# Layer-norm reciprocal deviation: square root on ScalarE and reciprocal on VectorE, in place of logarithm and exponential on ScalarE

## The chip, the cores and the metric

The kernel runs on one core of one Trainium2 chip. The metric is the device time of one launch in microseconds (us), median of several runs. Lower is better.

## The reference

One step of a two-layer streaming encoder over 1024 prompt tokens and 32 sample tokens (1056 columns together), model width 1024, all in float32. Layer 0 is a gated DeltaNet mixer and a convolutional feed-forward network (FFN), layer 1 is multi-head latent attention and an FFN of the same shape. Each of the four sub-layers ends in the same way, and that is what the change touches:

```
x = layer_norm(ALPHA * x + (1 + gate) * mix, ln_g, ln_b)

def layer_norm(x, g, b):
    mu = mean(x);  var = mean(square(x - mu))       # over the 1024 features
    return (x - mu) * rsqrt(var + 1e-5) * g + b
```

The next sub-layer reads `hin = x * (1 + scale) + shift` with its own conditioning terms.

## The kernel before, in words

The residual stream X stays in SBUF with features on the partitions: 8 blocks of 128 features by 1056 columns. The columns are worked in three chunks of 352 (`CHS`, ch = 0, 1, 2). Chunk 2 holds the last 320 prompt columns and the 32 sample columns, so an operation with a gain per sequence is issued twice there. Each float32 product on TensorE is three passes over a high and a low part (WH, WL of the weights, HH, HL of the activations, lines 374, 377 and 378).

The order of the work is written out by hand for each engine, and semaphores tie the engines together. No planner reorders it. Weights arrive on SyncE's DMA queue in slabs of 1024 columns (RAW), ScalarE rounds them to WH (`split_hi`, line 365), and GpSimd or VectorE forms WL (`split_lo`, line 370).

The four layer norms are q = 0 (after the DeltaNet), 1 (after the first FFN), 2 (after attention) and 3 (after the second FFN, at the end of the program). For q = 0, 1, 2 the first products of the next sub-layer follow at once. One norm works like this, chunk by chunk:

- `pe_mean` (lines 495 and 498): a product with a matrix of ones puts the column sum on all partitions, from partial sums that GpSimd has added (`pool_sum`, line 619) and the last block of X, which VectorE has just updated (`update` in `vec_proj`, line 1634, or in `vec_ffn`, line 2154).
- `vec_center` (line 640): VectorE subtracts the mean, two blocks at a time.
- `act_squares` (line 537): ScalarE squares, and `pe_var` (line 506) sums the squares, 8 products by a chunk.
- `act_rstd` (lines 539 to 545): ScalarE takes Ln of variance plus eps, waits for itself, and takes Exp of minus half of it. The semaphore `std_rdy` counts two steps for each chunk, 6 for each norm. The tile LN_R stands in the profile as RST.
- `vec_scaled` (lines 651 and 655): VectorE multiplies the centred X by gain and LN_R, which gives the tile TBN (q < 3) or X (q = 3). It waits for the second step of `std_rdy`.
- q < 3: `act_upper` (line 555) makes HH from TBN, `vec_low` (line 677) makes HL from TBN and HH. TensorE's next products of that chunk (`pe_head`) wait for both.
- q = 3: `vec_shift` (line 665) and `act_affine` (line 572) add the offset, and SyncE stores y.

On VectorE the order in `vec_tail` is, for q < 3: the updates of chunk 2, with the centring of chunk 1 among them or ahead of them. Then the first four blocks of `vec_scaled(0)`, *and only then* the last update of chunk 2. Then the rest of `vec_scaled(0)`, a weight slab, `vec_low(0)`, a second slab, the centring of chunk 2, and for chunks 1 and 2 in turn `vec_scaled` and `vec_low`. For q = 3 all updates come first, then two blocks of `vec_scaled(0)`, the centring of chunk 2, the other six blocks, `vec_shift(0)`, and `vec_scaled` and `vec_shift` of chunks 1 and 2.

On TensorE `pe_tail` puts the variance of chunk 0 in chunk 2 of the last products, then the mean of chunk 2 and the variance of chunk 1. `pe_head` starts the next sub-layer, with the variance of chunk 2 after its first product of chunk 0.

The latent projections of layer 1 (`rms_root`, line 2364, and `vec_norm`, line 2403) already take their reciprocal deviation as Sqrt on ScalarE and a reciprocal on VectorE, on the same 128 x 352 float32 shape.

Of the kernel before, what the change touches and what calls it, by code (L numbers as in the profile page):

```python
# [7 lines left out]
D = 1024  # L8
# [4 lines left out]
CHS = [(0, 352), (352, 352), (704, 352)]  # L13
# [95 lines left out]
def build(nc, xT, cT, cB, ws, wada0, wada, par, cst, s0, cs, msk, pckv, pkpe, y, o_gdn, o_gcv, s_gdn, o_fcv, o_ckv, o_kpe):  # L109
    fp32, f32r = mybir.dt.float32, mybir.dt.float32r  # L110
    ALU, ACT, AX = mybir.AluOpType, mybir.ActivationFunctionType, mybir.AxisListType
    ds = bass.ds
    ctx = ExitStack()
    with ctx:
# [13 lines left out]
        def sb(name, shape, dt=fp32):  # L128
            return at(name, shape, dt)[0]
# [3 lines left out]
        def sem(name):  # L133
            sems[name] = ctx.enter_context(nc.semaphore(name))
            return sems[name]
# [14 lines left out]
        EPS = sb("EPS", [128, 3])  # L150
# [70 lines left out]
        LN_SQ, LN_TB, LN_R, LN_SUM = [], [], [], []  # L221
# [32 lines left out]
        for i in range(3):  # L254
# [36 lines left out]
        PS = ctx.enter_context(nc.psum_tensor("PS", [128, 8, 512], fp32))  # L291
# [33 lines left out]
        sum_rdy, mean_ps, cen_rdy, lsq_rdy, var_ps, std_rdy, nrl_rdy, x_rdy = (sem(n) for n in (  # L325
            "sum_rdy", "mean_ps", "cen_rdy", "lsq_rdy", "var_ps", "std_rdy", "nrl_rdy", "x_rdy"))
# [40 lines left out]
        def split_lo(e, n, u):  # L367

            need(e, hi_done, n + 1)
            e.tensor_tensor(WL[u][:, :], RAW[:, u, :], WH[u][:, :].bitcast(fp32), ALU.subtract).then_inc(lo_done, 1)  # L370
# [39 lines left out]
        def pieces(c0, cw):  # L410

            out = []
            for st, (a, b) in enumerate((PRO, SAMP)):
                lo, hi = max(a, c0), min(b, c0 + cw)
                if lo < hi:
                    out.append((lo, hi - lo, st))
            return out
# [68 lines left out]
        def slab_after(q):  # L486

            return (S_F0, S_KV, S_F1, None)[q]
# [50 lines left out]
        def act_rstd(a, q, ch):  # L539

            cw = CHS[ch][1]
            a.wait_ge(var_ps, 3 * q + ch + 1)
            a.activation(LN_R[q][ch][:, 0:cw], PS[:, 3 + ch, 0:cw], ACT.Ln, scale=1.0 / D, bias=EPS[:, 0:1]).then_inc(std_rdy, 1)
            a.wait_ge(std_rdy, 6 * q + 2 * ch + 1)
            a.activation(LN_R[q][ch][:, 0:cw], LN_R[q][ch][:, 0:cw], ACT.Exp, scale=-0.5).then_inc(std_rdy, 1)

        def act_upper(a, q, ch):

# [29 lines left out]
        def act_ln(a, q):  # L578

            n = slab_after(q)  # L580
            act_squares(a, q, 0)
            act_rstd(a, q, 0)
            act_squares(a, q, 1)
            if q == 3:
                act_squares(a, q, 2)
                act_rstd(a, q, 1)
                act_affine(a, q, 0)
                act_rstd(a, q, 2)
                act_affine(a, q, 1)
                act_affine(a, q, 2)  # L590
                return
            split_hi(a, n, n % 2)
            act_upper(a, q, 0)
            split_hi(a, n + 1, (n + 1) % 2)
            act_rstd(a, q, 1)
            act_squares(a, q, 2)
            act_upper(a, q, 1)
            act_rstd(a, q, 2)
            act_upper(a, q, 2)
# [34 lines left out]
        def vec_center(v, q, ch, b):  # L634

            c0, cw = CHS[ch]
            if b == 0:
                v.wait_ge(mean_ps, 3 * q + ch + 1)
                mixed(v, q, KB - 1, ch)
            v.scalar_tensor_tensor(X[:, b:b + 2, c0:c0 + cw], PS[:, ch, 0:cw].unsqueeze(1).to_broadcast([128, 2, cw]), -1.0 / D,  # L640
                                   X[:, b:b + 2, c0:c0 + cw], ALU.mult, ALU.add).then_inc(cen_rdy, 1)

        def vec_scaled(v, q, ch, b0, b1):

            c0, cw = CHS[ch]
            hs = HS[q]
            v.wait_ge(std_rdy, 6 * q + 2 * ch + 2)
            v.wait_ge(cen_rdy, 12 * q + 4 * ch + 4)
            for b in range(b0, b1):
                if q == 3:  # L650
                    ins = v.scalar_tensor_tensor(X[:, b, c0:c0 + cw], X[:, b, c0:c0 + cw], PAR[:, P_LNG + KB * q + b:P_LNG + KB * q + b + 1],
                                                 LN_R[q][ch][:, 0:cw], ALU.mult, ALU.mult)
                else:
                    for x, w, st in pieces(c0, cw):
                        ins = v.scalar_tensor_tensor(LN_TB[q][ch][:, b, x - c0:x - c0 + w], X[:, b, x:x + w],
                                                     LGB[:, MODE[hs], 0, b, st:st + 1], LN_R[q][ch][:, x - c0:x - c0 + w], ALU.mult, ALU.mult)
                if b % 2 == 1:
                    ins.then_inc(nrl_rdy if q == 3 else tmp_rdy, 1)

        def vec_shift(v, ch):  # L660

            c0, cw = CHS[ch]
            v.wait_ge(nrl_rdy, 6 + 5 * ch + 4)
            for b in range(KB // 2, KB):
                ins = v.tensor_scalar(X[:, b, c0:c0 + cw], X[:, b, c0:c0 + cw], PAR[:, P_LNB + KB * 3 + b:P_LNB + KB * 3 + b + 1], None, ALU.add)
            ins.then_inc(nrl_rdy, 1)

        def vec_low(v, q, ch):

            c0, cw = CHS[ch]  # L670
            hs = HS[q]
            for b in range(KB):
                if b % 2 == 0:
                    v.wait_ge(hh_rdy, hin_count(hs, ch) - 3 + b // 2)
                    v.wait_ge(tmp_rdy, tmp_count(hs, ch) - 3 + b // 2)
                for x, w, st in pieces(c0, cw):
                    ins = v.scalar_tensor_tensor(HL[:, b, x:x + w], LN_TB[q][ch][:, b, x - c0:x - c0 + w], LGB[:, MODE[hs], 1, b, st:st + 1],
                                                 HH[:, b, x:x + w].bitcast(fp32), ALU.add, ALU.subtract)
            ins.then_inc(hl_rdy, 1)

        def vec_tail(v, q, update, groups, cut, first=iter(())):

            for ch in range(NCH):
                for i in range(groups):
                    if ch == 2 and i == groups - 1 and q < 3:
                        vec_scaled(v, q, 0, 0, 4)
                    update(ch, i)
                    if ch == 0:
                        next(first, None)
                        continue  # L690
                    if groups == 2 and i == 0:
                        for b in range(0, KB, 2):
                            vec_center(v, q, ch - 1, b)
                    elif groups == KB and 1 <= i <= 4:
                        vec_center(v, q, ch - 1, 2 * (i - 1))
                for _ in first:
                    pass
            if q == 3:
                vec_scaled(v, q, 0, 0, 2)
                for b in range(0, KB, 2):  # L700
                    vec_center(v, q, 2, b)
                vec_scaled(v, q, 0, 2, KB)
                vec_shift(v, 0)
                for ch in (1, 2):
                    vec_scaled(v, q, ch, 0, KB)
                    vec_shift(v, ch)
                return
            n = slab_after(q)
            vec_scaled(v, q, 0, 4, KB)
            split_lo(v, n, n % 2)  # L710
            vec_low(v, q, 0)
            split_lo(v, n + 1, (n + 1) % 2)
            for b in range(0, KB, 2):
                vec_center(v, q, 2, b)
            for ch in (1, 2):
                vec_scaled(v, q, ch, 0, KB)
                vec_low(v, q, ch)

# [232 lines left out]
        def past(e, s, count):  # L951

            if count > 0:
                e.wait_ge(s, count)
# [1152 lines left out]
        def vec_ffn(v, l, s, g0):  # L2107
# [233 lines left out]
            mix(NP - 2, beside())  # L2341
            last_lower(1, 0)
            vec_tail(v, 2 * l + 1, lambda ch, m: update(NP - 1, KB * ch + m, m, ch, last_bank), KB, 2, within())

        def no_hin(ch):
# [1146 lines left out]
```

## Time and profile before

| | |
|---|---|
| median of 3 runs | 3078.75 us |
| runs | 3074.51 to 3082.51 us |
| profiled execution, its own time | 3073.38 us |
| its span | 3071.6 us |
| TensorE busy | 95% of the span |
| VectorE busy | 74% |
| ScalarE busy | 40% |
| GpSimd busy | 36% |
| mean granted TensorE clock | 0.98 |

The span runs from the first to the last instruction of the profiled execution. Engines work side by side, so their shares don't add up to 100%. In the rows below a timeline merges like instructions in sequence into one row, and gives in brackets the time the engine sat idle before it and whose work ended that idle time.

### The profile page before, as it was taken

Reading aid. Unit: us, or ns where it says so; the run is one execution under the profiler, and the core shown is the slowest. Engines: PE = TensorE matmul, PEld = TensorE weight load, DVE = VectorE, ACT = ScalarE, POOL = GpSimd, SP = SyncE. Lnnn points to the kernel's source line nnn. Section 1 sums busy time; section 2 is a strip of 40 time slices with the busy share of each in tenths; the row PEclk is TensorE's granted clock in tenths of the full one; section 3 lists DMA queues with packets and bytes.
Section 4 is the critical chain, followed back from the end, with each engine's and each line's share of the span. In section 5 each row is a group of like instructions: output and inputs, shape, how many; then the busy total and the mean of one; then the engine's idle time right before and its main releaser. Section 6 shows DMA issues by size and latency. Waiting matters only on the chain.

```text
span 3071.6 us, 51912 instructions
## 1 busy us (share of the span) xinstructions
PE 2921.7 (95%) x18516; PEld 2795.7 (91%) x18516; DVE 2266.1 (74%) x3438; ACT 1218.5 (40%) x2348; POOL 1099.6 (36%) x727
## 2 busy tenths in 40 slices
PE   7999989999999999999999888989999999999997
PEld 5999986999898999999998877878889999999996
DVE  7999975777629788788787655646348778878777
ACT  4333334555416433333333644444346333333334
POOL 2333444666332344433344121111223433334432
PEclk9999989999999999999999999999999999999999
DMA  7454663211111111111111210101211111111111
GB/s 274 166 183 171 215 226 114 64 52 34 36 42 41 43 48 48 52 44 48 48 48 36 96 53 29 36 22 71 85 35 35 49 55 41 51 44 48 49 54 58
DMA packets 87017, 225.75 MB, mean 73 GB/s; under 512 B 9436, under 2 KB 41124, under 8 KB 85860
## 3 DMA queue, kind: packets, MB, share of 16 engines
q1 hardware_dynamic: 46948, 139.10, 13.2%
q10 hardware_dynamic: 39936, 84.86, 8.0%
q8 instruction: 85, 1.39, 0.2%
q14 instruction: 48, 0.39, 0.0%
HBM read 192.59 MB, written 31.35 MB: 73 GB/s over the span
## 4 chain that ended last, share of the span: by engine, by line
PE 77%; DVE 11%; issue 5%; ACT 4%; DMA 1%; ACTq 1%; POOL 0%; SPq 0%; DVEq 0%; POOLq 0%
PE PS L374 14%; PE PS L377 13%; PE PS L378 13%; PE PS L1735 6%; PE PS L1739 6%; PE PS L1738 6%; DVE CV L3292 4%; PE PS L981 2%; PE PS L2600 2%; PE PS L997 2%; PE PS L506 2%; DVE PS L861 1%; PE PS L2584 1%; PE PS L1053 1%; DVE X L2154 1%
## 5 line engine op out<-in xcount | busy, mean ns | idle before, releaser
L370 POOL TENSOR_TENSOR WL<-RAW,WH 128x1024 fp32r<-128x1024 f32 x193 | 508.7, 2636 | 1029.4 <-ACT WH L365 1029.3
L374 PE MATMUL PS<-HH,WH 128*128 128x352 f32 x2120 | 701.4, 331 | 38.4 <-issue 13.0
L378 PE MATMUL PS<-HH,WL 128*128 128x352 f32 x2120 | 688.2, 325 | 0.0
L377 PE MATMUL PS<-HL,WH 128*128 128x352 f32 x2120 | 687.5, 324 | 0.0
L374 PEld LDWEIGHTS PS<-HH,WH 128*128 128x128 f32 x2120 | 403.5, 190 | 55.9 <-issue 44.7
L377 PEld LDWEIGHTS PS<-HL,WH 128*128 128x128 f32 x2120 | 404.6, 191 | 1.8
L378 PEld LDWEIGHTS PS<-HH,WL 128*128 128x128 f32 x2120 | 403.8, 190 | 0.0
L365 ACT ACTIVATE WH<-RAW 128x1024 fp32r<-128x1024 f32 x199 | 210.4, 1057 | 461.7 <-PE PS L374 360.7
L2154 DVE SCALAR_TENSOR_TENSOR X<-PS,ADA,X 128x352 f32<-128x352 f32 (+1 forms) x704 | 319.2, 485 | 88.0 <-PE PS L378 83.6
L378 PE MATMUL PS<-FH,WL 128*128 128x352 f32 x960 | 310.7, 324 | 0.0
L374 PE MATMUL PS<-FH,WH 128*128 128x352 f32 x960 | 310.4, 323 | 0.0
L377 PE MATMUL PS<-FL,WH 128*128 128x352 f32 x960 | 310.3, 323 | 0.0
L2126 DVE SCALAR_TENSOR_TENSOR CF<-UF,PSF,CF 128x1060 f32<-128x1060 f32 x176 | 291.2, 1709 | 0.0
L861 DVE CUSTOM_DVE_ANT_0 PS<-ADR,CB 128x1024 f32<-128x1024 f32 x144 | 196.6, 1365 | 6.8 <-DMA ADR<-wada 2.3
L374 PEld LDWEIGHTS PS<-FH,WH 128*128 128x128 f32 x960 | 180.6, 188 | 0.3
L377 PEld LDWEIGHTS PS<-FL,WH 128*128 128x128 f32 x960 | 180.5, 188 | 0.0
L378 PEld LDWEIGHTS PS<-FH,WL 128*128 128x128 f32 x960 | 180.0, 187 | 0.0
L1557 POOL TENSOR_TENSOR AM<-M,CST 128x1024 f32<-128x1024 f32 (+1 forms) x61 | 135.7, 2241 | 69.3 <-PE PS L981 50.7
L3292 DVE SCALAR_TENSOR_TENSOR CV<-U,PST,CV 128x1060 f32<-128x1060 f32 x72 | 139.8, 1942 | 17.1 <-ACT CV L3129 15.4
L1735 PE MATMUL PS<-HH,WH 128*128 128x352 f32 x456 | 148.1, 325 | 4.1 <-issue 4.1
L1739 PE MATMUL PS<-HH,WL 128*128 128x352 f32 x456 | 147.8, 324 | 0.0
L1738 PE MATMUL PS<-HL,WH 128*128 128x352 f32 x456 | 147.6, 324 | 0.0
(389 smaller groups left out, 6286.0 us busy)
## 6 DMA issues: line engine op xcount, KB each, us to landing
RAW<-ws SPq DMA_DIRECT2D x199, 512.0 KB, 3.3
ADR<-wada ACTq DMA_DIRECT2D x72, 512.0 KB, 4.7
scr<-V ACTq DMA_DIRECT2D x32, 528.0 KB, 3.0
X<-xT SPq DMA_DIRECT2D x3, 1408.0 KB, 20.7
OUTT<-scr SPq DMA_DIRECT2D x1, 4224.0 KB, 15.5
y<-X SPq DMA_DIRECT2D x6, 704.0 KB, 4.8
AD0R<-wada SPq DMA_DIRECT2D x8, 512.0 KB, 13.0
AD<-wada SPq DMA_DIRECT2D x2, 2048.0 KB, 14.9
```

The lines of the kernel that those rows point to most:

```text
L365: e.activation(WH[u][:, :], RAW[:, u, :], ACT.Copy).then_inc(hi_done, 1)
L370: e.tensor_tensor(WL[u][:, :], RAW[:, u, :], WH[u][:, :].bitcast(fp32), ALU.subtract).then_inc(lo_done, 1)
L374: mm = e.matmul(out, WH[w][:, c:c + 128], mh, start=first, stop=False)
L377: e.matmul(out, WH[w][:, c:c + 128], ml, start=False, stop=False)
L378: return e.matmul(out, WL[w][:, c:c + 128], mh, start=False, stop=last)
L861: ins = v.tensor_tensor_reduce(out=PS[:, B_ADA:B_ADA + 2, :].rearrange("p b c -> p (b c)"), in0=ADR[:, 3 * u + q, :], in1=CB[:, st, :], sc ...
L1735: mm = e.matmul(out, lhs, xh[:, r + k, c0:c0 + CW], start=first and k == 0, stop=False, skip_group_check=not first)
L1738: e.matmul(out, lhs, xl[:, r + k, c0:c0 + CW], start=False, stop=False, skip_group_check=not first)
L1739: mm = e.matmul(out, wl[:, c + 128 * k:c + 128 * k + 128], xh[:, r + k, c0:c0 + CW], start=False, stop=k == 3, skip_group_check=not first)
L2126: ins = v.scalar_tensor_tensor(CF[:, half, :], src, w, CF[:, half, :], ALU.mult, ALU.add)
L2154: ins = v.scalar_tensor_tensor(X[:, m, a:a + w], PS[:, bank_(k), a - c0:a - c0 + w], ADA[:, s, 2 * KB + m, st:st + 1], X[:, m, a:a + w], A ...
L3292: v.scalar_tensor_tensor(CV[u][:, :], src(j), PST[:, u, j:j + 1], CV[u][:, :], ALU.mult, ALU.add)\
```

## The change

`act_rstd` keeps its first ScalarE operation, with Sqrt in place of Ln. Its second one (Exp) is gone, and a new function `vec_rstd` takes a reciprocal on VectorE in place, as the second step of `std_rdy`. It is called ahead of the first `vec_scaled` of each chunk, so 12 times in all. `past` is a wait that is left out where the count is 0. It makes ScalarE's Sqrt of a chunk wait until VectorE's reciprocal of the chunk before is done, which keeps the count of `std_rdy` in order.

```
@@ -540,9 +540,14 @@
             cw = CHS[ch][1]
             a.wait_ge(var_ps, 3 * q + ch + 1)
-            a.activation(LN_R[q][ch][:, 0:cw], PS[:, 3 + ch, 0:cw], ACT.Ln, scale=1.0 / D, bias=EPS[:, 0:1]).then_inc(std_rdy, 1)
-            a.wait_ge(std_rdy, 6 * q + 2 * ch + 1)
-            a.activation(LN_R[q][ch][:, 0:cw], LN_R[q][ch][:, 0:cw], ACT.Exp, scale=-0.5).then_inc(std_rdy, 1)
+            past(a, std_rdy, 6 * q + 2 * ch)
+            a.activation(LN_R[q][ch][:, 0:cw], PS[:, 3 + ch, 0:cw], ACT.Sqrt, scale=1.0 / D, bias=EPS[:, 0:1]).then_inc(std_rdy, 1)
+
+        def vec_rstd(v, q, ch):
+
+            cw = CHS[ch][1]
+            v.wait_ge(std_rdy, 6 * q + 2 * ch + 1)
+            v.reciprocal(LN_R[q][ch][:, 0:cw], LN_R[q][ch][:, 0:cw]).then_inc(std_rdy, 1)
@@ -683,6 +688,7 @@
                     if ch == 2 and i == groups - 1 and q < 3:
+                        vec_rstd(v, q, 0)
                         vec_scaled(v, q, 0, 0, 4)
                     update(ch, i)
@@ -696,12 +702,14 @@
             if q == 3:
+                vec_rstd(v, q, 0)
                 vec_scaled(v, q, 0, 0, 2)
...
                 for ch in (1, 2):
+                    vec_rstd(v, q, ch)
                     vec_scaled(v, q, ch, 0, KB)
                     vec_shift(v, ch)
                 return
@@ -713,6 +721,7 @@
             for ch in (1, 2):
+                vec_rstd(v, q, ch)
                 vec_scaled(v, q, ch, 0, KB)
                 vec_low(v, q, ch)
```

## Rows read from the trace of the kernel before

**Rows 1.** The page's busy times by engine, and its chain by engine.

```profile
PE 2921.7 (95%) x18516; PEld 2795.7 (91%) x18516; DVE 2266.1 (74%) x3438; ACT 1218.5 (40%) x2348; POOL 1099.6 (36%) x727
...
PE 77%; DVE 11%; issue 5%; ACT 4%; DMA 1%; ACTq 1%; POOL 0%; SPq 0%; DVEq 0%; POOLq 0%
```

**Rows 2.** Instructions of lines 543 and 545: duration min/median/max ns, first and last start.

```profile
L543 ACT ACT_TABLE_LOAD  x12: 1283/1283/1283, 910.2 to 3056.6; - x12
L543 ACT ACTIVATE RST<-PS,EPS x12: 554/556/558, 914.6 to 3057.9; 128x352 f32<-128x352 f32 x12
...
L545 ACT ACT_TABLE_LOAD  x12: 1283/1283/1283, 915.2 to 3058.4; - x12
L545 ACT ACTIVATE RST<-RST x12: 496/497/500, 916.5 to 3059.7; 128x352 f32<-128x352 f32 x12
```

**Rows 3.** The same view of lines 2403 and 2364, in the latent projections.

```profile
L2403 DVE RECIPROCAL RSM<-RSM x6: 2339/2349/2355, 1777.8 to 1804.3; 128x352 f32<-128x352 f32 x6
...
L2364 ACT ACT_TABLE_LOAD  x1: 1283/1283/1283, 1774.9 to 1774.9; - x1
```

**Rows 4.** VectorE's timeline there: start, us, line, idle before and releaser.

```profile
1777.76 2.35 DVE L2403 RECIPROCAL RSM<-RSM 128x352 f32<-128x352 f32 x1 [1.20 <-ACT RSM L2364]
1780.14 3.27 DVE L2406 SCALAR_TENSOR_TENSOR CKF<-CKF,PAR,RSM 128x352 f32<-128x352 f32 x2
```

**Rows 5.** VectorE's timeline in the norm q = 0.

```profile
922.81 2.06 DVE L655 SCALAR_TENSOR_TENSOR TBN<-X,LGB,RST 128x352 f32<-128x352 f32 x4
924.79 0.70 DVE L1634 SCALAR_TENSOR_TENSOR X<-PS,ADA,X 128x320 f32<-128x320 f32 x2
...
936.83 4.04 DVE L655 SCALAR_TENSOR_TENSOR TBN<-X,LGB,RST 128x352 f32<-128x352 f32 x8
940.79 4.04 DVE L677 SCALAR_TENSOR_TENSOR HL<-TBN,LGB,HH 128x352 fp32r<-128x352 f32 x8
946.09 5.09 DVE L655 SCALAR_TENSOR_TENSOR TBN<-X,LGB,RST 128x320 f32<-128x320 f32 x16 [1.26 <-ACT RST L545]
951.11 5.08 DVE L677 SCALAR_TENSOR_TENSOR HL<-TBN,LGB,HH 128x320 fp32r<-128x320 f32 x16
```

**Rows 6.** TensorE's timeline in the norm q = 0, all its stops.

```profile
925.55 0.86 PE L495 MATMUL PS<-SUMX,CST 128*128 128x352 f32 x2 [2.12 <-DVE X L1634]
...
956.29 0.40 PE L374 MATMUL PS<-HH,WH 128*128 128x352 f32 x1 [2.82 <-issue]
```

**Rows 7.** ScalarE's timeline in the norm q = 0, chunks 1 and 2.

```profile
933.46 0.56 ACT L543 ACTIVATE RST<-PS,EPS 128x352 f32<-128x352 f32 x1 [2.64 <-PE PS L506]
...
943.70 0.56 ACT L543 ACTIVATE RST<-PS,EPS 128x352 f32<-128x352 f32 x1
```

**Rows 8.** VectorE's timeline in the norm q = 1.

```profile
1685.12 3.03 DVE L655 SCALAR_TENSOR_TENSOR TBN<-X,LGB,RST 128x352 f32<-128x352 f32 x4
...
1710.38 5.09 DVE L655 SCALAR_TENSOR_TENSOR TBN<-X,LGB,RST 128x320 f32<-128x320 f32 x16 [2.22 <-ACT RST L545]
```

**Rows 9.** GpSimd's timeline in the norm q = 1, its last sums.

```profile
1684.66 2.12 POOL L619 TENSOR_TENSOR SUMC<-SUMC,X 128x352 f32<-128x352 f32 x2 [0.47 <-DVE X L2154]
```

**Rows 10.** VectorE's timeline in the norm q = 2.

```profile
2304.46 5.09 DVE L655 SCALAR_TENSOR_TENSOR TBN<-X,LGB,RST 128x320 f32<-128x320 f32 x16 [1.26 <-ACT RST L545]
```

**Rows 11.** VectorE's timeline in the norm q = 3.

```profile
3045.10 1.07 DVE L651 SCALAR_TENSOR_TENSOR X<-X,PAR,RST 128x352 f32<-128x352 f32 x2
3046.86 3.28 DVE L640 SCALAR_TENSOR_TENSOR X<-PS,X 128x704 f32<-128x704 f32 x4 [0.69 <-PE PS L498]
...
3054.68 4.05 DVE L651 SCALAR_TENSOR_TENSOR X<-X,PAR,RST 128x352 f32<-128x352 f32 x8 [0.19 <-ACT RST L545]
...
3060.27 4.05 DVE L651 SCALAR_TENSOR_TENSOR X<-X,PAR,RST 128x352 f32<-128x352 f32 x8 [0.16 <-ACT RST L545]
```

**Rows 12.** Windows: busy time by engine, granted TensorE clock, DMA share, GB/s.

```profile
923.00:930.00 7.00, 4.88 (x12) 2.79 (x11) 7.00 (x14) 6.98 (x12) 0.00 (x0) 0.76 0.03 4
953.00:961.00 8.00, 5.18 (x23) 4.92 (x23) 7.96 (x20) 1.67 (x4) 0.00 (x0) 0.79 0.01 2
```

More of the change, by code:

```diff
@@ L542, in act_rstd, with vec_rstd @@
             a.wait_ge(var_ps, 3 * q + ch + 1)
-            a.activation(LN_R[q][ch][:, 0:cw], PS[:, 3 + ch, 0:cw], ACT.Ln, scale=1.0 / D, bias=EPS[:, 0:1]).then_inc(std_rdy, 1)
-            a.wait_ge(std_rdy, 6 * q + 2 * ch + 1)
-            a.activation(LN_R[q][ch][:, 0:cw], LN_R[q][ch][:, 0:cw], ACT.Exp, scale=-0.5).then_inc(std_rdy, 1)
+            past(a, std_rdy, 6 * q + 2 * ch)
+            a.activation(LN_R[q][ch][:, 0:cw], PS[:, 3 + ch, 0:cw], ACT.Sqrt, scale=1.0 / D, bias=EPS[:, 0:1]).then_inc(std_rdy, 1)
+        def vec_rstd(v, q, ch):
+            cw = CHS[ch][1]
+            v.wait_ge(std_rdy, 6 * q + 2 * ch + 1)
+            v.reciprocal(LN_R[q][ch][:, 0:cw], LN_R[q][ch][:, 0:cw]).then_inc(std_rdy, 1)
         def act_upper(a, q, ch):
@@ L685, in vec_tail @@
                     if ch == 2 and i == groups - 1 and q < 3:
+                        vec_rstd(v, q, 0)
                         vec_scaled(v, q, 0, 0, 4)
@@ L698, in vec_tail @@
             if q == 3:
+                vec_rstd(v, q, 0)
                 vec_scaled(v, q, 0, 0, 2)
@@ L704, in vec_tail @@
                 for ch in (1, 2):
+                    vec_rstd(v, q, ch)
                     vec_scaled(v, q, ch, 0, KB)
@@ L715, in vec_tail @@
             for ch in (1, 2):
+                vec_rstd(v, q, ch)
                 vec_scaled(v, q, ch, 0, KB)
```

## The prediction

> **What bounds the kernel now.** I read the page's busy shares first, then its chain of waits. TensorE is busy for 95% of the span and carries 77% of the chain, VectorE carries 11%, ScalarE 4% [rows 1]. Over the whole kernel ScalarE has time to spare, and freeing some is worth nothing by itself. But the change lives in four short stretches, the norms, and there the average says little. So I then read the timelines of each engine inside a norm, looking for who is never idle. In q = 0 it is VectorE: from 922.81 us to the end of the norm at 956.2 us the only gap is 1.26 us ahead of chunk 2's `vec_scaled`, waiting for ScalarE's Exp [rows 5]. TensorE stops twice in the same stretch, 2.12 us for VectorE's last update of X, which stands *behind* the first half of `vec_scaled(0)` in program order, and 2.82 us ahead of the product that starts at 956.29 us, just after `vec_low(2)` ends at 951.11 + 5.08 = 956.19 us [rows 5, 6]. The second is named "issue" in the row, but its end coincides with HL of chunk 2, which that product reads. So in a norm VectorE's queue sets the pace, and TensorE waits for it. The same pattern holds in q = 1 and q = 2, with gaps of 2.22 and 1.26 us ahead of chunk 2 [rows 8, 10]. In q = 3, the end of the program, nothing but the norm is left. VectorE has gaps of 0.69 us (for the mean of chunk 2), 0.19 and 0.16 us (for Exp), and its last `vec_scaled` and `vec_shift` are followed only by the store of y [rows 11].
>
> **What the change removes.** Per chunk ScalarE loses the Exp (0.497 us) and the table load ahead of it (1.283 us), 1.78 us, and for most chunks the load ahead of Ln too, since nothing brings another table in between [rows 2]. The nearest evidence that Sqrt needs one load for a run of chunks is the latent projections, where six Sqrt with squares and copies between them took one load [rows 3]. That is 12 x 1.78 + 8 x 1.283 = 31.6 us of ScalarE time with one load for each norm. What lies on the path of it is small: VectorE's waits for Exp, 1.26, 2.22, 1.26, 0.19 and 0.16 us, in all 5.09 us.
>
> The Trainium skill (ScalarE: Activation LUTs, Table sets) says that Ln and Exp share a set, one load for both. By that, the change would save ScalarE only the 0.497 us of each Exp. This trace does not agree: a load of 1.283 us stands ahead of each of the 12 Exp [rows 2].
>
> **What the change adds.** Twelve reciprocals of 128 x 352 float32 on VectorE. The same operation on the same shape took 2.349 us (median of 6) [rows 3]. What counts is how far it pushes the next instruction, which waits for the reciprocal's own semaphore: in the latent projections the next one started 1780.14 - 1777.76 = 2.38 us after it [rows 4]. A busy VectorE starts an instruction about 0.08 us before the recorded end of the last (924.79 against 922.81 + 2.06 = 924.87) [rows 5], so the bounds are 2.35 - 0.08 = 2.27 us if the self-wait is free, and about 2.4 us. I take 2.38 us, the direct row. Three in a norm are 7.14 us, 12 are 28.6 us. By the same overlap, a gap that disappears is worth its idle time plus 0.08 us.
>
> **q = 0.** The first reciprocal comes at 922.81 us. Its Sqrt, at Ln's place (914.6 us [rows 2]), is done long before, so no wait. Behind it are half of `vec_scaled(0)` and then the last update, for which TensorE already waits, so TensorE's stop grows from 2.12 to 4.50 us. From there on everything up to `vec_low(0)` and the centring of chunk 2 is 2.38 us late. The second reciprocal stands where `vec_scaled(1)` started, at 936.83 + 2.38 = 939.21 us. Is its Sqrt there? Ln started at 933.46 us, right behind the variance [rows 7], which is 2.38 us late too, and Sqrt takes Ln's 0.556 us: ready at 936.4 us, in time. `vec_scaled(1)` and `vec_low(1)` are then 4.76 us late, and VectorE reaches chunk 2 at 940.79 + 4.04 - 0.08 + 4.76 = 949.5 us. The third Sqrt stands behind `act_upper(1)` on ScalarE. Ln started there at 943.70 us, right behind its load [rows 7], so `act_upper(1)` ended at 942.4 us. It reads what `vec_scaled(1)` writes and is up to 4.76 us late, so Sqrt ends by 942.4 + 4.76 + 0.56 = 947.7 us. That is in time as well: the gap of 1.26 us goes, and the reciprocal takes its place. Net 3 x 2.38 - (1.26 + 0.08) = **5.80 us**. The added wait on ScalarE (`past`) holds Sqrt of chunk 2 until the second reciprocal ends at about 941.6 us, with `act_upper(2)` queued behind it: too early to matter. TensorE may get a new stop ahead of chunk 1, whose HL is 4.76 us late where TensorE is 2.38 us late, but that is hidden because it still reaches chunk 2 before VectorE has its HL ready.
>
> **q = 1.** The same three, and a gap of 2.22 + 0.08 = 2.30 us goes. There is one more term. The first half of `vec_scaled(0)` took 3.03 us, against 2.06 us for the same four in q = 0, while GpSimd was adding X from 1684.66 to 1686.78 us [rows 5, 8, 9]. With the reciprocal in front, these four start at about 1687.5 us, after GpSimd is done. If the reciprocal itself isn't stretched, 0.97 us comes back. The bounds are 0 and 0.97. I take 0.97: net 7.14 - 2.30 - 0.97 = **3.87 us** (4.84 at the other bound).
>
> The Trainium skill (SBUF — State Buffer, SBUF: two separate sides) has a VectorE instruction with two SBUF inputs contend with GpSimd's reads; a reciprocal has one input. The stretched row agrees, and by the rule the 0.97 us comes back; without it the kernel's sum would be 1 us more.
>
> **q = 2.** As q = 0: 7.14 - (1.26 + 0.08) = **5.80 us**.
>
> **q = 3.** The reciprocal of chunk 0 comes after all updates, so the mean isn't delayed, and it fills the 0.69 us gap. The centring of chunk 2 is 2.38 - 0.77 = 1.61 us late. Chunk 1: before, Exp's result came at about 3054.6 us. Now the squares ahead are 1.6 us late, but 1.283 + 1.283 + 0.497 us of loads and Exp are gone: about 3053.2 us, while VectorE gets there only at 3054.68 - 0.27 + 1.61 = 3056.0 us. Chunk 2: Sqrt waits through `past` until the reciprocal of chunk 1 ends at 3058.4 us. Queued behind are the offsets of chunk 1, whose inputs don't exist sooner than 3059.5 us. VectorE needs that Sqrt at 3063.8 us. All three gaps go: 7.14 - (0.69 + 0.19 + 0.16 + 3 x 0.08) = **5.86 us**, and the stores are later by that.
>
> **Sum.** 5.80 + 3.87 + 5.80 + 5.86 = 21.3 us. The profiled execution took 3073.38 us (span 3071.6 and 1.8 around it), so its like should take 3094.7 us. It lay 5.4 us under the median of the runs, 3078.75, and I forecast against that: **3100.1 us**. Between the norms TensorE's products run almost unbroken, and all that feeds them hangs on semaphores and not on absolute time, so I see nothing that gives the delay back. The load at line 2364 goes too if Sqrt's table stays; I take it at 0 because it stands ahead of a wait for TensorE; VectorE waited 1.20 us for that Sqrt [rows 4], the most that it could give.
>
> **Rivals.**
> *A, ScalarE decides and the kernel gets faster.* Place: chunk 2's `vec_scaled`, waiting for Exp in all of q = 0, 1, 2, and chunks 1 and 2 of q = 3. Price: 5.1 + 5 x 0.08 = 5.5 us, and the three TensorE stops before chunk 2 would shrink with it, saving up to 1.7 us of half clock each (0.24 x 7 us and 0.21 x 8 us of the granted clock missing around such stops [rows 12]). That gives 3078.75 - 5.5 - 5.1 = 3068 us. It decides if a reciprocal costs VectorE less than 5.5 / 12 = 0.46 us, or if VectorE's queue had such room. For it: those waits are real. Against it: 2.35 us in six rows, and a queue with hardly a gap. The Trainium skill (ScalarE: Activation LUTs, What ACT_TABLE_LOAD costs) puts a set switch at 2.66 us with a drain of 1.38 us, which would speak for this side. Here the first load ahead of Exp starts at 915.2 us and its Exp at 916.5 us, 1.283 us on [rows 2], with no room for a drain.
>
> *B, given back in the FFNs.* The delays of q = 0 and q = 2 come ahead of hundreds of microseconds in which ScalarE, GpSimd and DMA have slack. If TensorE were held there by something that the delay leaves in place (a weight slab), those 11.6 us would vanish: 3.87 + 5.86 = 9.7 us stay, 3088.5 us. Against it: TensorE stands at 95%, and its own products can't be caught up.
>
> *C, the clock adds to it.* Each TensorE stop in a norm is followed by a stretch at the lower level, 1.2 GHz: 1.7 us lost around each [rows 12]. My sum hides the longer first stop and the new one ahead of chunk 1. If both cost that much unhidden in three norms: 3 x 2 x 1.7 = 10 us more, 3110 us. Against it: VectorE, not TensorE, is late after each.
>
> That the Sqrt table is loaded at every chunk after all (the change not doing what it says) would cost nothing: at 1.28 us more, every Sqrt is still in time.
>
> **Chances.** Forecast 0.72, A 0.03, B 0.12, C 0.10, and 0.03 for what I don't see. About 0.3%, 9.2 us, is what a measurement can tell from no change: the runs alone spread by 8 us. Slower by more than that: the forecast, C and over half of B, 0.87. Within it: 0.09. Faster: 0.04. The range takes half of B and most of C, the bounds of the reciprocal (12 x 0.11 = 1.3 us down), the 1 us of q = 1, and 4 us for the runs' median: 3090 to 3108 us.
>
> **What would show it.** Twelve reciprocals at 2.35 us. ScalarE down by some 30 us busy, with four or so Sqrt loads. VectorE up by 28 us. Time from the first `vec_scaled` of q = 0 to the end of its `vec_low(2)` 33.4 + 5.8 us. TensorE's stop ahead of the mean of chunk 2 at 4.5 us. Half of `vec_scaled(0)` in q = 1 at 2.1 us. I am wrong if VectorE waits for Sqrt ahead of a reciprocal, if the reciprocal's length depends on data or on GpSimd, or if the FFN stretches between the norms change length by microseconds.

## The result and the profile after

The changed kernel is slower, as forecast, by somewhat less than forecast on its first timing.

| | median, us | ratio to before, 95% interval |
|---|---|---|
| before, runs beside it | 3076.83 (3066.97 to 3082.51) | |
| changed kernel | 3093.17 (3090.72 to 3100.66) | 1.006 [1.0039, 1.008] |
| changed kernel, timed again (below) | 3095.50 | 1.0081 [1.0058, 1.0105] |

The forecast was 3100.1 us, 21.3 us over before, a ratio of 1.0069. That lies inside both intervals. Between the medians there are 16.3 us on the first timing and 24.8 us on the second, so the timings alone don't tell 21.3 from its neighbours. The forecast's 3100.1 us is 6.9 us over the measured 3093.17: 1.9 us of that is the median of before that it started from (3078.75, against 3076.83 with three more runs), 5.0 us the difference itself. The profiled execution of the changed kernel has a span of 3088.9 us against 3071.6, so 17.3 us more.

The page after, busy times by engine. ScalarE lost 31.4 us (forecast some 30), VectorE gained 26.6 (forecast 28), TensorE's work is the same.

```profile
PE 2923.2 (95%) x18516; PEld 2796.6 (91%) x18516; DVE 2292.7 (74%) x3450; ACT 1187.1 (38%) x2315; POOL 1101.3 (36%) x727
```

The instructions on the tile of the reciprocal deviation after (duration min/median/max ns, first and last start), and the table loads from the groups by line (count, busy us, mean ns, idle before). They answer to [rows 2, 3]: the reciprocal takes what it took in the latent projections, and there are 4 loads for the 12 Sqrt, one for each norm.

```profile
L544 ACT ACTIVATE RST<-PS,EPS x12: 533/554/557, 911.4 to 3072.1; 128x352 f32<-128x352 f32 x12
L550 DVE RECIPROCAL RST<-RST x12: 2341/2348/2352, 919.6 to 3077.4; 128x352 f32<-128x352 f32 x12
```

```profile
L544 ACT ACT_TABLE_LOAD x4 | 5.1, 1283 | 0.1
```

VectorE's timeline after in q = 0, against [rows 5]. The gap of 1.26 us ahead of chunk 2 is gone, and three reciprocals stand in a queue with no other hole.

```profile
919.61 2.34 DVE L550 RECIPROCAL RST<-RST 128x352 f32<-128x352 f32 x1
921.99 2.07 DVE L660 SCALAR_TENSOR_TENSOR TBN<-X,LGB,RST 128x352 f32<-128x352 f32 x4
...
936.01 2.35 DVE L550 RECIPROCAL RST<-RST 128x352 f32<-128x352 f32 x1
938.39 4.06 DVE L660 SCALAR_TENSOR_TENSOR TBN<-X,LGB,RST 128x352 f32<-128x352 f32 x8
942.37 4.05 DVE L682 SCALAR_TENSOR_TENSOR HL<-TBN,LGB,HH 128x352 fp32r<-128x352 f32 x8
946.33 2.35 DVE L550 RECIPROCAL RST<-RST 128x352 f32<-128x352 f32 x1
948.72 5.09 DVE L660 SCALAR_TENSOR_TENSOR TBN<-X,LGB,RST 128x320 f32<-128x320 f32 x16
953.73 5.08 DVE L682 SCALAR_TENSOR_TENSOR HL<-TBN,LGB,HH 128x320 fp32r<-128x320 f32 x16
```

TensorE's stops after in the same norm, against [rows 6]: 2.12 us became 4.50, there is a new one ahead of chunk 1, and the one ahead of chunk 2 grew from 2.82 to 4.47.

```profile
924.74 1.54 PE L495 MATMUL PS<-SUMX,CST 128*128 128x352 f32 x2 [4.50 <-DVE X L1643]
946.52 0.40 PE L374 MATMUL PS<-HH,WH 128*128 128x352 f32 x1 [0.53 <-issue]
958.91 0.63 PE L374 MATMUL PS<-HH,WH 128*128 128x352 f32 x1 [4.47 <-issue]
```

VectorE's timeline after in q = 1, against [rows 8]: the four operations behind the first reciprocal take 2.07 us and no longer 3.03.

```profile
1688.41 2.34 DVE L550 RECIPROCAL RST<-RST 128x352 f32<-128x352 f32 x1
1690.78 2.07 DVE L660 SCALAR_TENSOR_TENSOR TBN<-X,LGB,RST 128x352 f32<-128x352 f32 x4
```

VectorE's timeline after in q = 3, against [rows 11].

```profile
3058.74 2.34 DVE L550 RECIPROCAL RST<-RST 128x352 f32<-128x352 f32 x1
...
3069.66 2.35 DVE L550 RECIPROCAL RST<-RST 128x352 f32<-128x352 f32 x1
...
3077.40 2.35 DVE L550 RECIPROCAL RST<-RST 128x352 f32<-128x352 f32 x1
3079.78 4.06 DVE L656 SCALAR_TENSOR_TENSOR X<-X,PAR,RST 128x352 f32<-128x352 f32 x8
3083.87 1.34 DVE L670 TENSOR_SCALAR X<-X,PAR 128x352 f32<-128x352 f32 x4
```

**Where the time went.** The table cuts the span at instructions of VectorE. A norm (q = 0, 1, 2) runs from the first reciprocal, or without one from the first `vec_scaled`, to the start of `vec_low(2)`. For q = 3 it ends with the start of the last `vec_shift`, and the tail is the rest of the span. All in us, from each kernel's own profile. The two right-hand columns are the repeats of the next section.

| | before | changed | difference | before again | changed again |
|---|---|---|---|---|---|
| ahead of q = 0 | 922.81 | 919.61 | -3.20 | 922.17 | 920.42 |
| q = 0 | 28.30 | 34.12 | +5.82 | 27.88 | 34.10 |
| between | 734.01 | 734.68 | +0.67 | 732.44 | 734.54 |
| q = 1 | 30.27 | 34.11 | +3.84 | 29.28 | 34.11 |
| between | 565.77 | 565.96 | +0.19 | 565.22 | 565.70 |
| q = 2 | 28.31 | 34.12 | +5.81 | 27.89 | 34.11 |
| between | 735.63 | 736.14 | +0.51 | 733.95 | 736.21 |
| q = 3 | 19.26 | 25.13 | +5.87 | 19.25 | 25.11 |
| tail | 7.24 | 5.03 | -2.21 | 7.22 | 5.10 |
| span | 3071.6 | 3088.9 | +17.3 | 3065.3 | 3089.4 |

The four norms grew by 21.34 us, where the sum had 21.33. What the sum didn't have are the stretches around them: 3.2 us less ahead of the first norm, 1.4 us more between the norms, 2.2 us less in the tail. Nearly all of the 3.2 us was there before TensorE's first mean for this norm, at 904.7 us: VectorE's update of X at 879.83 us in the profile of before starts at 876.66 us in that of the changed kernel, 3.17 us sooner.

### The profile page after: what moved, and what is told of

It is laid out like the page before. It is cut to its first block, busy times and chain, and to the rows that moved or that the text cites. A ratio compares the mean times of both kernels' runs of the same rounds, so it can differ in the third digit from the quotient of the medians.

```text
span 3088.9 us, 51902 instructions
## 1 busy us (share of the span) xinstructions
PE 2923.2 (95%) x18516; PEld 2796.6 (91%) x18516; DVE 2292.7 (74%) x3450; ACT 1187.1 (38%) x2315; POOL 1101.3 (36%) x727
## 3 DMA queue, kind: packets, MB, share of 16 engines
q8 instruction: 85, 1.39, 0.2%
## 4 chain that ended last, share of the span: by engine, by line
PE 73%; DVE 14%; issue 6%; ACT 4%; DMA 1%; ACTq 1%; POOL 0%; SPq 0%; DVEq 0%; POOLq 0%
PE PS L374 13%; PE PS L377 13%; PE PS L378 13%; PE PS L1744 6%; PE PS L1748 6%; PE PS L1747 6%; DVE CV L3301 4%; PE PS L990 2%; PE PS L2609 2%; PE PS L1006 2%; DVE PS L870 1%; PE PS L2593 1%; PE PS L1062 1%; DVE X L2163 1%; DVE RST L550 1%
```

## Experiments

All were timed beside the kernel before, e0 to e3 on one chip and e4 to e7 on another. Before had a median of 3070.72 us beside the first four and 3072.22 us beside the rest, so runs of the two groups are compared by their ratios to it.

**The kernel before again (e0_before), no edit.**

> The kernel before once more, to see which stretches move between profiles of the same program. The changed kernel's profile was 17.3 us longer: four norms +5.82, +3.84, +5.81, +5.87, the stretches between them +0.67, +0.19, +0.51, the stretch ahead of the first norm -3.20 and the stretch behind the last offset -2.21. If the -3.2 us ahead of the first norm is scatter, this profile puts the first norm somewhere between 915 and 925 us and not at 922.8 again. Norms repeat within 0.1 us; the tail from the last VectorE offset (start) to the end of the span stays 7.2 us. Ratio 1.000.

Ratio 0.9996 [0.9984, 1.0009], median 3068.80 us. Its profile is in the table. Two of my expectations failed. The first norm came at 922.17 us again, so the 3.2 us ahead of it are not shown to be scatter. And the first three norms did not repeat within 0.1 us: they were 0.4 to 1.0 us shorter, and the stretches behind q = 0 and q = 2 1.6 us shorter. The windows say why. These are the rows of this repeat (busy by engine, then the granted TensorE clock, DMA share, GB/s), around the same two stops of 2.12 and 2.92 us:

```profile
920.00:930.00 10.00, 7.88 (x35) 5.84 (x34) 10.00 (x19) 9.97 (x15) 0.00 (x0) 1.00 0.06 13
950.00:962.00 12.00, 9.08 (x58) 8.82 (x57) 11.93 (x29) 5.27 (x13) 0.94 (x1) 1.00 0.01 2
```

And the same windows of the first profile of before:

```profile
920.00:930.00 10.00, 7.88 (x31) 5.79 (x30) 10.00 (x18) 9.44 (x15) 0.50 (x5) 0.83 0.02 3
950.00:962.00 12.00, 9.18 (x48) 8.92 (x47) 11.93 (x31) 4.72 (x15) 0.00 (x0) 0.86 0.01 2
```

The same program kept TensorE at 2.4 GHz through both stops in one execution, and in the other TensorE fell to 1.2 GHz for a while: the mean of 0.83 lies between the two levels, 1.00 and 0.50.

**The changed kernel again (e1_after), no edit.**

> The changed kernel once more, beside the one before on the same chip. My theory, the sum of the four norms 21.3 us, plus some 0.55 us of TensorE clock for each of three norms, less 2.2 us given back by the queue of the stores of y: +20.8 us, ratio 1.0067. If instead 4 us of it are really given back in the stretch ahead of the first norm: +16.5 us, ratio 1.0054. Tail 5.0 us.

Ratio 1.0081 [1.0058, 1.0105], 24.8 us between the medians. The lower of my two numbers, 1.0054, is outside. Its norms repeat within 0.03 us, its tail is 5.10 us, and its windows around the stops are low again, 0.73 and 0.77. The same windows of its first profile:

```profile
918.00:930.00 12.00, 7.50 (x23) 5.14 (x23) 11.96 (x20) 8.52 (x14) 0.00 (x0) 0.72 0.06 15
955.00:970.00 15.00, 10.68 (x50) 10.45 (x51) 11.54 (x27) 4.63 (x11) 2.38 (x1) 0.77 0.01 1
```

Against the profile of before whose clock held at those two stops, the spans differ by 24.1 us: +23.13 in the norms, +4.84 between them, -1.75 ahead and -2.12 in the tail. The fastest runs of the two kernels differ by as much, 24.0 us here (3090.41 and 3066.45) and 23.8 us on the first timing (3090.72 and 3066.97).

**ScalarE's half alone (e2_no_recip).**

```
-            past(a, std_rdy, 6 * q + 2 * ch)
-            a.activation(..., ACT.Sqrt, ...).then_inc(std_rdy, 1)
+            a.activation(..., ACT.Sqrt, ...).then_inc(std_rdy, 2)
...
-            v.wait_ge(std_rdy, 6 * q + 2 * ch + 1)
-            v.reciprocal(...).then_inc(std_rdy, 1)
+            v.wait_ge(std_rdy, 6 * q + 2 * ch + 2)
```

> The ScalarE half alone: Sqrt in place of Ln and Exp, no reciprocal on VectorE, and no wait for it (the reciprocal is left out of the computation). My theory: only VectorE's waits for Exp go, 1.34, 2.30, 1.34 and 0.43 us, so -5.4 us against before, of which the queue of stores takes up to 0.4 us back: 0.998 to 0.9985. Rival A in full, with TensorE's clock recovered at its shorter stops: -10 us, 0.9967. If ScalarE's 31 us counted: -31 us, 0.990.

Ratio 0.9961 [0.9948, 0.9973], median 3060.47 us: 10 us faster. That is the size that rival A gave and nearly twice my own number. Its span is 6.4 us below that of e0: the norms -0.93, -1.35, -0.92, -0.53, the tail -2.16, the rest between. So ScalarE's 31 us are worth 3.7 us in the norms, and 2.2 us at the very end, where I hadn't looked. The rest of the 10 us is probably how often the clock holds, which is not separated: of its 12 timed runs one was above 3061.1 us, with mean clocks of 0.982 to 0.984, where before's lay between 3066 and 3081 us, with 0.978 to 0.984. The reciprocal is left out of the computation here. e7 below leaves nothing out and has the same four norms within 0.03 us.

**The reciprocal twice (e3_twice).**

```
             v.reciprocal(LN_R[q][ch][:, 0:cw], LN_R[q][ch][:, 0:cw]).then_inc(std_rdy, 1)
+            v.wait_ge(std_rdy, 6 * q + 2 * ch + 2)
+            v.reciprocal(LN_SUM[q][ch][:, 0:cw], LN_R[q][ch][:, 0:cw])
```

> The reciprocal done twice at each of the 12 places (the second copy goes to an unused tile). My theory, VectorE's queue is the path through all four norms and nothing later gives time back: 12 x 2.3 = +27 to +28.5 us against the changed kernel, +48 us against before, ratio 1.0155. Rival B, delays of q = 0 and q = 2 given back in the FFNs: +14 us against the changed kernel. Rival C, a longer TensorE stop costs clock in proportion: +28 and another 3 to 10 us.

Ratio 1.0151 [1.013, 1.0172], median 3119.01 us, 23.5 us over e1 by the medians and 25.6 by the spans. Each of the four norms grew by 6.49 to 6.52 us over e1, 26.0 in all, and 25.6 of that reach the end of the span, so what VectorE's queue takes on shows in full. Rival B (half given back, +14 us) is excluded. A clock cost that grows with the stop doesn't show either: TensorE's first stop is 6.68 us here against 4.50, and the stretches between the norms are 1.2 us shorter in all. A second reciprocal costs 2.17 us, below my 2.3: its successor doesn't wait for it, and `vec_scaled` behind it ran a little shorter. VectorE's timeline of this kernel in q = 0, chunk 1:

```profile
939.81 2.34 DVE L550 RECIPROCAL RST<-RST 128x352 f32<-128x352 f32 x1
942.18 2.35 DVE L552 RECIPROCAL SUMX<-RST 128x352 f32<-128x352 f32 x1
944.45 3.96 DVE L662 SCALAR_TENSOR_TENSOR TBN<-X,LGB,RST 128x352 f32<-128x352 f32 x8
```

**The change in the last norm only (e4_end_only).**

```
 def act_rstd:   +if q < 3: Ln, wait, Exp as before; return
 def vec_rstd:   +if q < 3: return
```

> The change in the last norm (q = 3) alone, Ln and Exp in the other three. My theory now: VectorE is 5.87 us later there, and the time from its last offset to the end of the span falls from 7.2 to 5.1 us, because ScalarE's offsets of chunk 1 no longer stand behind the loads and the Exp of chunk 2, so the stores of y are issued sooner: +3.7 us, ratio 1.0012. Rival, the tail is scatter or depends on the earlier norms: tail 7.2 us and +5.9 us, ratio 1.0019. The profile tells them apart.

Ratio 1.0018 [1.0004, 1.0031], median 3077.95 us. The timing can't tell 3.7 from 5.9 us (the fastest runs of each lie 3.4 us apart), the profile can: q = 3 took 25.12 us (+5.86) and the tail 5.02 us. q = 0 and q = 2 took 28.30 us, as in the first profile of before, q = 1 28.86 us against 30.27 and 29.28 there, though nothing was changed in it (on that below). The tail is shorter because of the change in the last norm. The mechanism stands in ScalarE's queue. Before, chunk 1's offsets (the first four of these eight) stand behind the loads, Ln and Exp of chunk 2:

```profile
3058.45 1.28 ACT L545 ACT_TABLE_LOAD   x1
3059.74 0.50 ACT L545 ACTIVATE RST<-RST 128x352 f32<-128x352 f32 x1
3060.15 3.92 ACT L572 ACTIVATE X<-X,PAR 128x352 f32<-128x352 f32 x8
```

In e4 only chunk 2's Sqrt stands ahead of them, they start 0.5 us behind it, when VectorE has their input, and chunk 2's come 7.7 us later:

```profile
3053.72 0.55 ACT L549 ACTIVATE RST<-PS,EPS 128x352 f32<-128x352 f32 x1 [3.53 <-DVE RST L557]
3054.78 2.06 ACT L584 ACTIVATE X<-X,PAR 128x352 f32<-128x352 f32 x4 [0.50 <-DVE X L663]
3062.51 2.06 ACT L584 ACTIVATE X<-X,PAR 128x352 f32<-128x352 f32 x4 [5.67 <-DVE X L663]
```

Each store of half a chunk of y waits on SyncE for its offsets, and the four last ones ran into each other before: they were issued from 3062.2 to 3065.7 us. In e4 the six issues spread from 3050.2 to 3066.9 us. The stores' rows of before and of e4, with the time from issue to landing:

```profile
L3009 SPq DMA_DIRECT2D y<-X x6: 372/389/507, 3056.6 to 3065.7; - x6
...
DMA to landing us min/median/max: 3.4/4.8/5.5
```

```profile
L3025 SPq DMA_DIRECT2D y<-X x6: 372/372/405, 3050.2 to 3066.9; - x6
...
DMA to landing us min/median/max: 3.3/3.3/4.1
```

**The first reciprocal of q = 0 and q = 2 in VectorE's idle time (e5_early).**

```
+                    if (ch, i) == (2, 0) and q in (0, 2):
+                        vec_rstd(v, q, 0)
                     if ch == 2 and i == groups - 1 and q < 3:
-                        vec_rstd(v, q, 0)
+                        if q == 1:
+                            vec_rstd(v, q, 0)
```

> The changed kernel with the first reciprocal of q = 0 and q = 2 moved ahead of VectorE's first update of chunk 2, into its idle time of 8 us there (the others stay). Theory: the two norms fall from 34.1 to 31.7 us, TensorE's first stop there from 4.5 to 2.1 us; -4.8 us against the changed kernel, and up to 1.5 us more each where TensorE's clock then survives the stop: -5 to -8 us, ratio to before about 1.005. Rival, the place in the queue doesn't matter since TensorE absorbs it: no difference from the changed kernel.

Ratio 1.0053 [1.0033, 1.0073], median 3091.66 us. The place does what it should: the reciprocal starts at 913.25 us in a hole, and TensorE's first stop is 2.12 us again (the one ahead of chunk 2 stays at 4.47).

```profile
913.25 2.35 DVE L550 RECIPROCAL RST<-RST 128x352 f32<-128x352 f32 x1 [4.74 <-ACT RST L544]
916.48 0.71 DVE L1646 SCALAR_TENSOR_TENSOR X<-PS,ADA,X 128x320 f32<-128x320 f32 x2 [0.88 <-PE PS L378]
```

From the first `vec_scaled` (920.87 us) to `vec_low(2)` (952.59) it is 31.72 us, where the changed kernel took 34.12 from its reciprocal on. But the profiled execution had a span of 3096.1 us, 6.7 more than e1: its stretches behind q = 0 and q = 2 took 740.1 and 741.5 us, where e1's took 734.5 and 736.2. GpSimd's weight splits were longer in it (2.72 us against 2.63). I have no experiment on that. This execution was also the second slowest of the six. The gain of 2.4 us in each of the two norms is shown. That it reaches the end of the program is not: the profile has it lost again behind the norms, and the timings give 0.28% between two intervals that overlap, on two chips (the fastest run is 3085.06 us, e1's 3090.41). So the rival, that the place in the queue makes no difference to the time, stands open.

**A short operation in the reciprocal's place (e6_cheap).**

```
-            v.reciprocal(LN_R[q][ch][:, 0:cw], LN_R[q][ch][:, 0:cw]).then_inc(std_rdy, 1)
+            v.tensor_scalar(LN_R[q][ch][:, 0:cw], LN_R[q][ch][:, 0:cw], 1.0, None, ALU.mult).then_inc(std_rdy, 1)
```

> The changed kernel with a plain multiply by 1 in place of the reciprocal, at the same places with the same waits (the reciprocal is left out of the computation). By the length of such VectorE operations it costs 0.3 to 0.45 us a piece. Theory, rival A's threshold of 0.46 us: 12 x 0.4 = 4.8 us less the 5.4 us of waits, less 2.1 us of tail: -3 us against before, ratio 0.999, and TensorE's first stop at 2.5 us. If waiting for its own semaphore or the ordering with ScalarE were what costs, and not the reciprocal's 2.35 us: several us slower than before.

Ratio 0.9975 [0.9961, 0.9988], median 3065.75 us: 6.5 us faster than before, twice what I expected; the fastest runs lie 3.0 us apart (3063.84 and 3066.79). The row of the operation, and TensorE's first stop, 2.50 us as expected:

```profile
L550 DVE TENSOR_SCALAR RST<-RST x12: 330/341/711, 921.0 to 3054.4; 128x352 f32<-128x352 f32 x12
```

```profile
924.15 1.51 PE L495 MATMUL PS<-SUMX,CST 128*128 128x352 f32 x2 [2.50 <-DVE X L1643]
```

So the place, the two waits and the ordering through `past` are cheap. It is the reciprocal's 2.35 us for 352 columns, seven times a multiply's 0.34, that turns a gain into a loss. But the gain of this kernel doesn't come from the norms. They take 28.09, 29.09, 28.09 and 19.48 us, 1.39 us less in all than in the first profile of before and 0.45 us more than in the second. Its tail is 5.09 us, 2.1 us shorter than in either, and that is the part which is sure.

**One ScalarE function for both (e7_one_function), as e2, with another function.**

```
-            a.activation(..., ACT.Sqrt, ...).then_inc(std_rdy, 1)
+            a.activation(..., ACT.Abs_reciprocal_sqrt, ...).then_inc(std_rdy, 2)
...              (no reciprocal, no wait through past)
```

> A version meant to beat both: ScalarE takes the reciprocal square root in one function (Abs_reciprocal_sqrt), with no Exp, no second load and nothing on VectorE. Theory: the same timing as the kernel without reciprocals, whose profile was 6.4 us shorter and whose median 10 us shorter than before: ratio 0.996 to 0.998, outputs complete. Rival: the function needs a load of its own at each chunk, then ScalarE has 12 loads, which still hide: 0.998.

Ratio 0.9948 [0.9932, 0.9964], median 3058.61 us: 13.6 us under before, more than I expected, and faster than both kernels. It leaves nothing of the computation out. It needs 4 table loads in place of 24. They stand after the wait for the variance here, with the chunk's sum done, so 1.28 us of load is on ScalarE's path of chunk 0, where VectorE has time.

```profile
L543 ACT ACT_TABLE_LOAD x4 | 5.1, 1283 | 20.5 <-PE PS L506 20.5
```

```profile
923.58 1.40 PE L495 MATMUL PS<-SUMX,CST 128*128 128x352 f32 x2 [2.12 <-DVE X L1641]
953.00 0.40 PE L374 MATMUL PS<-HH,WH 128*128 128x352 f32 x1 [1.52 <-issue]
```

Its norms take 26.93, 27.94, 26.94 and 18.71 us, its tail 5.05, and TensorE's stop ahead of chunk 2 is 1.52 us. The norms are e2's within 0.03 us; that the profile's span is 2.4 us under e2's lies for the most part ahead of the first norm (1.9 us), where the two kernels do the same.

## Why the prediction was right, point by point

**VectorE's queue sets the pace in a norm.** Right, and shown: e3 adds to it, and the norms and the span grow by what it adds (26.0 and 25.6 us); e2 and e7 take the waits out of it, and the norms shorten by 0.5 to 1.4 us each against the second profile of before. e6 puts 0.34 us in the place of 2.35, and the norms are 22.7 us shorter than those of the changed kernel.

**The sum of the norms.** Forecast 5.80, 3.87, 5.80, 5.86, measured 5.82, 3.84, 5.81, 5.87 against the profile that it was worked out from. The reciprocal's step of 2.38 us is confirmed (919.61 to 921.99). Every gap went as forecast, each Sqrt was in time, and TensorE's first stop is 4.50 us to the digit. The 0.97 us of q = 1 came back: the four operations behind the reciprocal took 2.07 us. The load at line 2364 went too, and VectorE's wait behind it stayed at 1.20 us, so 0 was the right term. The agreement is better than the method deserves, since the second profile of before has other norms: against that one the same sum would have been 23.2 us (measured 23.1), because VectorE's gaps ahead of chunk 2 are shorter there, 0.84, 1.25 and 0.85 us. The gap goes with TensorE's clock, probably since TensorE's products, the variance of chunk 2 among them, end sooner at the higher level. In q = 1, unchanged in all three, it was 2.22, 1.25 and 0.84 us (before, before again, e4), and the granted clock in the first part of the norm 0.79, 0.89 and 1.00:

```profile
1684.00:1700.00 16.00, 12.86 (x45) 8.88 (x45) 16.00 (x28) 10.31 (x15) 2.17 (x3) 0.79 0.19 66
1681.00:1697.00 16.00, 12.84 (x52) 9.26 (x51) 16.00 (x29) 10.94 (x16) 2.54 (x3) 0.89 0.19 59
1683.00:1699.00 16.00, 11.90 (x54) 8.89 (x54) 16.00 (x28) 12.58 (x18) 2.17 (x3) 1.00 0.20 66
```

That the forecast of 21.3 us lies between the two measured differences is in part luck: against the second profile of before, the norms (+1.8 us over the sum) and the stretches between them (+4.8) missed one way, the tail (-2.1) and the stretch ahead (-1.8) the other.

**"I see nothing that gives the delay back."** Right for the FFNs as far as e1 and e3 go, wrong for the tail. I had left the stores of y as "later by that". The 2.2 us were to be had from [rows 11] and ScalarE's timeline: the loads and the Exp of chunk 2 delayed chunk 1's offsets, and so bunched the stores. It is the one place outside the norms where ScalarE's freed time pays (e2, e4, e6, e7 all show a tail of 5.0 to 5.1 us).

**Rival C, the clock, at 0.10.** It was not all or nothing. Against the first profile of before, which had lost the clock at its short stops already, the stretches behind the longer stops are 0.67, 0.19 and 0.51 us longer. In q = 0 TensorE restarts wholly at the lower level (granted clock 0.50 from 924.7 to 930.0 us), where before it fell after the restart (0.62 from 925.5 to 930.0 us). Against the execution in which the clock had held, the stretches between are 2.10, 0.48 and 2.26 us longer, 4.8 in all. That is the last of the signs under which I had said I would be wrong, stretches that change by microseconds, and the sum has no term for it. I had read one profile and taken its clock for the program's. What is shown is the granted clock of these executions. That the clock makes up the rest of the run-to-run spread of before is likely from the runs' mean clocks (0.984 in the fastest, 0.978 in the slowest), but not separated.

**Rival A, faster, at 0.03.** Its premise, that the waits for Exp are real, was right (e2), and the price of the reciprocal decides: with 0.34 us in its place the kernel is faster. Its threshold of 0.46 us is not shown. With the waits of the second profile of before (0.84, 1.25, 0.85, 0.18 and 0.15 us) its own formula gives 3.67 / 12 = 0.31 us, a multiply pushed its successor by 0.37 us, and e6's norms neither gain nor lose clearly. What is sure of e6's gain is the tail, which the rival didn't have.

**Rival B** is excluded by e3. **That the table is loaded at each chunk** did not happen.

**Open.** The 3.2 us that the changed kernel's profile saved ahead of the first norm (1.75 in the repeat): the difference is there before the first instruction of the change runs, and e2, which has ScalarE's half of the change, starts its first norm at 922.71 us like the kernel before. Part of it may be the clock: from 818 to 838 us it was granted at 0.83 in both profiles of before and in e2, and at 0.91 in both of the changed kernel. And the FFN stretches, which range from 731 to 741 us over these profiles; the clock explains some 2 us of it, not the 5.5 us of e5.

## What to carry to other kernels

Price a moved operation on the engine that receives it, in the stretch where it lands, and compare with the wait it removes there: ScalarE got 31 us back, of which some 6 to 8 were on the path (4 to 6 in the norms, depending on which profile of before e2 is set against, and 2.2 in the tail); VectorE took on 28 us, and all but the 1 us of relief from GpSimd was. Look for one function that replaces the pair before splitting a pair over two engines. And take a second profile of the kernel before: stops of 2 to 3 us of TensorE came with and without a loss of clock in the same program, which moved the baseline by 6 us.

## What the runs showed of the hardware

- A VectorE reciprocal of 128 x 352 float32 took 2.34 to 2.35 us in all 12 places, also (2.34 us) in the one where GpSimd was adding beside it (q = 1, from 1688.41 us, GpSimd from 1687.95 to 1689.97 us). A multiply by a constant of the same shape took 0.34 us, and 0.71 us in that one place (e6). A fused multiply-multiply with two SBUF inputs went from 0.52 to 0.76 us each beside the same GpSimd sums (before, q = 1).
- One table load of 1.283 us served the three Sqrt of a norm with Square, Copy and Identity between them (4 loads for 12 Sqrt). Ln and Exp in turn took one each (24 for 12 pairs).
- Abs_reciprocal_sqrt on ScalarE took 0.556 us for 128 x 352, what Ln and Sqrt took.
- TensorE stopped for 2.12 and 2.92 us and kept 2.4 GHz in one execution. After stops of 2.12 and 2.82 us it ran at 1.2 GHz in another, and after the changed kernel's stops of 4.5 us it did so in both of its profiles.
